# The second layer's modulation taken from TensorE to VectorE

## The reference, cut to what matters

```python
for i in range(DEPTH):
    mod_l = jnp.split((jax.nn.silu(c) @ w_mod[i] + b_mod[i])[:, None, :], N_MOD, axis=-1)
    mod_c = jnp.split((jax.nn.silu(c_ctx) @ w_mod[i] + b_mod[i])[None, None, :], N_MOD, axis=-1)
    h_l = modulate(rms_norm(x, norm1_g[i]), mod_l[0], mod_l[1])
    ...
    x = x + mod_l[2] * y_l
    x = x + mod_l[5] * squared_relu_mlp(modulate(rms_norm(x, norm2_g[i]), mod_l[3], mod_l[4]),
                                        w_mlp1[i], w_mlp2[i])
```

## Time and profile before

| what | value |
|---|---|
| median of 3 runs | 3845.44 us (3844.76 to 3845.57) |
| profiled execution, its own time | 3846.0 us |
| its span | 3843.8 us |
| PE busy | 3704.2 us, 96% of the span |
| DVE busy | 1794.8 us, 47% |
| ACT busy | 1378.0 us, 36% |
| mean granted clock of PE | 0.988 |

### The profile page before, as it was taken

The page is one execution under the profiler, slowest core; times in us unless marked ns, Lnnn a source line. Parts: engine busy times, 40 slices in busy tenths (PEclk is TensorE's granted clock), DMA queues, the critical chain, the costliest instruction groups (busy, mean ns, idle before and its releaser), DMA issues.

```text
span 3843.8 us, 65162 instructions
## 1 busy us (share of the span) xinstructions
PE 3704.2 (96%) x27522; PEld 3347.2 (87%) x27522; DVE 1794.8 (47%) x3203; ACT 1378.0 (36%) x2720; POOL 471.8 (12%) x570
## 2 busy tenths in 40 slices
PE   7999899999999999999999999999998999999998
PEld 7877778888888887888899889999997988999998
DVE  4544555233233556644455564443345556444444
ACT  3544444122123444422322352342233235234322
POOL 1122211000002432100011100110012110011001
PEclk9999999999999999999999999999999999999999
DMA  5111122232321211222311112222221111222222
GB/s 186 71 62 51 62 76 72 101 114 100 114 105 53 73 55 58 77 99 94 112 53 55 50 50 91 86 83 84 93 83 45 45 56 53 94 86 88 89 94 72
DMA packets 88128, 306.08 MB, mean 80 GB/s; under 512 B 10000, under 2 KB 13200, under 8 KB 87712
## 3 DMA queue, kind: packets, MB, share of 16 engines
q1 hardware_dynamic: 85184, 293.25, 21.7%
q0 software_dynamic: 2656, 8.68, 0.7%
HBM read 299.79 MB, written 2.10 MB: 79 GB/s over the span
## 4 chain that ended last, share of the span: by engine, by line
PE 90%; DVE 4%; ACT 3%; POOL 1%; issue 1%; DMA 0%; SPq 0%; POOLq 0%; DVEq 0%; ACTq 0%
PE bank L576 65%; PE bank L638 6%; PE bank L607 2%; PE bank L1089 2%; PE bank L875 2%; PE bank L914 1%; PE bank L1075 1%; PE bank L733 1%; PE bank L820 1%; PE bank L942 1%; PE bank L967 1%; PE bank L954 1%; DVE weight_lo L1870 1%; PE bank L1185 1%; PE bank L1213 1%
## 5 line engine op out<-in xcount | busy, mean ns | idle before, releaser
L1870 DVE TENSOR_TENSOR weight_lo<-weight_raw,weight_hi 128x1024 fp32r<-128x1024 f32 (+1 forms) x464 | 558.1, 1205 | 553.8 <-ACT weight_hi L1282 553.6
L1282 ACT ACTIVATE weight_hi<-weight_raw 128x1024 fp32r<-128x1024 f32 (+1 forms) x464 | 477.0, 1031 | 614.8 <-PE bank L576 371.1
L576 PE MATMUL bank<-u_hi,weight_hi 128*128 128x256 f32 (+1 forms) x2112 | 611.5, 290 | 2.5 <-DVE weight_lo L1870 2.3
L576 PE MATMUL bank<-u_lo,weight_hi 128*128 128x256 f32 (+1 forms) x2112 | 599.0, 284 | 0.0
L576 PE MATMUL bank<-u_hi,weight_lo 128*128 128x256 f32 (+1 forms) x2112 | 598.3, 283 | 0.0
L576 PE MATMUL bank<-h_hi,weight_hi 128*128 128x512 f32 (+1 forms) x1328 | 486.0, 366 | 16.0 <-DVE h_lo L2284 9.2
L576 PE MATMUL bank<-h_lo,weight_hi 128*128 128x512 f32 (+1 forms) x1328 | 466.5, 351 | 0.0
L576 PE MATMUL bank<-h_hi,weight_lo 128*128 128x512 f32 (+1 forms) x1328 | 465.9, 351 | 0.0
L576 PEld LDWEIGHTS bank<-u_hi,weight_hi 128*128 128x128 f32 x2112 | 399.6, 189 | 26.3 <-issue 20.8
L576 PEld LDWEIGHTS bank<-u_hi,weight_lo 128*128 128x128 f32 x2112 | 399.4, 189 | 0.0
L576 PEld LDWEIGHTS bank<-u_lo,weight_hi 128*128 128x128 f32 x2112 | 398.4, 189 | 0.2
(11 more groups left out here) (279 smaller groups left out, 7352.8 us busy)
## 6 DMA issues: line engine op xcount, KB each, us to landing
weight_raw<-in_w_mlp SPq DMA_DIRECT2D x128, 512.0 KB, 3.5
weight_raw<-in_w_ff SPq DMA_DIRECT2D x128, 512.0 KB, 3.5
weight_raw<-in_w_in SPq DMA_DIRECT2D x92, 512.0 KB, 3.5
weight_raw<-in_w_mod SPq DMA_DIRECT2D x80, 512.0 KB, 4.4
weight_raw<-in_a_w_qkv SPq DMA_DIRECT2D x24, 512.0 KB, 3.6
weight_raw<-in_b_w_qkv SPq DMA_DIRECT2D x24, 512.0 KB, 3.5
first_weight<-in_w_mod SPq DMA_DIRECT2D x16, 512.0 KB, 15.2
weight_raw<-in_w_ret_o SPq DMA_DIRECT2D x16, 512.0 KB, 3.4
```

The source lines that it names most:

```text
L576: m = e.matmul(view[:, 0:hi - lo], a[:, k, :], b[:, k0 + k, lo:hi], start=(k == 0 and i == 0), stop=(k == kt - 1 and i == 2))
L1282: e.activation(whi[s % N_SPLIT][:, 0:kt, :], raw[n % N_RAW][:, 0:kt, :], ACT.Copy).then_inc(*tick("act_split", ("hi", n)))
L1870: e.tensor_tensor(wlo[s][:, 0:kt, :], raw[n % N_RAW][:, 0:kt, :], whi[s][:, 0:kt, :].bitcast(F32), ALU.subtract).then_inc(*tick("dve_split ...
```

## The change

The layer-1 modulation leaves PE. The weights of layer 1's modulation are laid out on the host so that a tile holds 128 output columns, one on each partition, and along it the 1024 weights of that output. DVE multiplies such a tile by a row that holds the activated vector (the same on every partition) and sums the products along the row (`accum_out`), once for `c` and once for `c_ctx`. The products themselves go to scratch for the first and over the raw tile for the second; only the sums are used. The rows (`vector_rows`, 1 MB) are loaded by POOL after the attention of layer 0 and activated by ACT in one instruction of 128 x 2048. The bias is added once at the end. The side turns are 53 instead of 56. On DVE, the side turn is taken in front of the work on the running product's bank instead of behind it. The last ACT wait is there because the scratch of the products is the rows of squares that layer 1's norm uses.

```diff
+        CROWS = sb("vector_rows", [P, 2, D], F32, o_lcl)
+        PRODUCT = SCR[:, 4:6, :].rearrange("p a b -> p (a b)")[:, 0:D]
...
+            def modulation_loads(layer):
+                for m in range(6 * KT):
+                    done_with[weight((f"w_mod{layer}", m), split=False)] = ("modp", layer, m)
+                    yield
...
-            last = diffusion_layer(0, modulation(0, 2 * KT, 6 * KT, True),
-                                   paced(modulation(1, 0, 6 * KT, False), 6 * KT, 56))
+            last = diffusion_layer(0, modulation(0, 2 * KT, 6 * KT, True), paced(modulation_loads(1), 6 * KT, 53))
...
+            def vector_rows():
+                e.wait_ge(*at("crows"))
+                e.activation(CROWS[:, :, :], CROWS[:, :, :], ACT.Silu).then_inc(*tick("act_mod", ("crowss",)))
...
                 attention_layer(layer, side1)
+                if layer == 0:
+                    vector_rows()
                 def finish(q, m, span):
                     if q == 3 and layer == 0:
+                        e.wait_ge(*at("modp", 1, 6 * KT - 1))
                         square(("n1", 1), m, span, x_all(m, N_ALL), "xm", layer, q, m)
...
+            def modulation_rows(layer):
+                e.wait_ge(*at("crowss"))
+                for m in range(6 * KT):
+                    n = number[f"w_mod{layer}", m]
+                    w = raw[n % N_RAW][:, :, :].rearrange("p k c -> p (k c)")
+                    e.wait_ge(*at("raw", n))
+                    e.wait_ge(*at("modp", layer, m - 1))
+                    for s, to in enumerate((PRODUCT, w)):
+                        e.scalar_tensor_tensor(out=to, in0=w, scalar=1.0, in1=CROWS[:, s, :], op0=ALU.mult, op1=ALU.mult,
+                                               accum_out=mod_row(layer, m, s)).then_inc(
+                            *tick("dve_mod", ("modp", layer, m)))
+                    if m + 1 < 6 * KT:
+                        yield
+                e.wait_ge(*at("modp", layer, 6 * KT - 1))
+                both = MOD[layer][:, :].rearrange("p (m s) -> p m s", s=2)
+                e.tensor_tensor(both, both, vec("b_mod", 48 * layer, 48).unsqueeze(2).to_broadcast([P, 48, 2]),
+                                ALU.add).then_inc(*tick("dve_mod", *(("modd", layer, m) for m in range(6 * KT))))
+                yield
...
                         split_ahead(number[w1, KT * q + m])
+                        if q or m >= TURN:
+                            next(side, None)
                         j = m % 2
                         e.wait_ge(*at("relu", name, q, m))
...
-                        if q or m >= TURN:
-                            next(side, None)
...
                         split_ahead(number[w2, KT * q + m])
+                        next(side, None)
                         for span in range(len(tok.spans)):
                             finish(q, m, span, tok)
-                        next(side, None)
...
+                if layer == 0:
+                    e.dma_start(CROWS[:, :, :].rearrange("p s k -> p (s k)"), t["c_rows"]).then_inc(
+                        *tick("dma_crows", ("crows",), by=16))
                 turn(("n2", layer), KT)
...
-        out[f"w_mod{i}"] = tiles_of(a["w_mod"][i])
+        out[f"w_mod{i}"] = np.ascontiguousarray(a["w_mod"][i].T.reshape(-1, P, D)) if i else tiles_of(a["w_mod"][i])
```

More of the change, by code:

```diff
@@ L496, in mod, with mod_row @@
             return MOD[layer][:, j:j + 1]
+        def mod_row(layer, m, s):
+            return MOD[layer][:, 2 * m + s:2 * m + s + 1]
         def source(key):
@@ L1391, in modulation @@
                     e.wait_ge(*at("modp", layer, m0 + 1))
-                    e.wait_ge(*(at("modq", layer, m0 - 2) if m0 else at("modq", layer - 1, 46)))
+                    e.wait_ge(*at("modq", layer, m0 - 2))
                     e.activation(ROWS, view_of("mod", layer, m0)[:, 0:2 * P], ACT.Copy).then_inc(
@@ L1829, in scalar_program @@
             first_norm()
-            diffusion_layer(0, modulation(0, 2 * KT, 6 * KT, True),
-                            paced(modulation(1, 0, 6 * KT, False), 6 * KT, 56))
+            diffusion_layer(0, modulation(0, 2 * KT, 6 * KT, True), ())
             m0, w = KT - TURN, "b_w_qkv"
@@ L2675, in vector_program @@
             first_norm()
-            diffusion_layer(0, modulation(0, 2 * KT, 6 * KT, True),
-                            paced(modulation(1, 0, 6 * KT, False), 6 * KT, 56))
+            diffusion_layer(0, modulation(0, 2 * KT, 6 * KT, True), paced(modulation_rows(1), 6 * KT, 53))
             m0, w = KT - TURN, "b_w_qkv"
@@ L3153, in layout @@
     out["lambdas"] = np.ascontiguousarray(np.broadcast_to(lam.reshape(1, -1), (P, 4 * HD)))
+    both = np.stack([a["c"].reshape(-1), a["c_ctx"].reshape(-1)])
+    out["c_rows"] = np.ascontiguousarray(np.broadcast_to(both.reshape(1, -1), (P, 2 * D)))
     rows = lambda x: np.ascontiguousarray(x.reshape(-1, KT, P).transpose(2, 1, 0))
```

## The result

| | before | changed kernel |
|---|---|---|
| median | 3845.51 us | 3796.41 us |
| range of the executions (4 each) | 3844.76 to 3845.85 | 3793.54 to 3800.40 |
| ratio, 95% interval | | 0.9872 (0.9859 to 0.9885) |
| profiled execution | 3846.0 us | 3793.54 us |
| its span | 3843.8 us | 3791.6 us |

The kernel became 49 us faster, 1.3%.

A forecast was written before the change was run, and what follows sets the result against it. PE was taken to bound the MLP of layer 0, busy 482.00 of 482.00 us. 3846.0 - 39.4 (work leaving PE) + 1.0 (waits) = 3807.6, the median 0.6 lower, so 3807; range 3803 to 3818.

The forecast's parts named there:

- What leaves PE: MLP of layer 0 on PE: removing layer 1's modulation tiles and turnings saves 39.4 us, with a product at 8.46.
- What DVE gets: 96 products of 128 x 1024 with sums on DVE, taken as 2.65 us per pair.
- the lower end: Lowest price for a tile's pair of products on DVE, with free sums: 2 x 1.20 = 2.4 us.
- The first rival: DVE, L2067: sums run at half rate, a pair takes 4.9 us; time 3902, slower by 56; chance 0.12.
- Whether DVE keeps up: DVE's turns in the MLP: load is no limit, order is; PE waits 1 us, from 0 to 8.
- the ring: Waits through the raw buffer: DVE pair, SP load, ACT, DVE split, next pair; 8.66 us against a product's 8.46.
- the ring falls behind by 0.2 us per turn: MLP: ring 8.66 against product 8.46 uses up a lead of 1.8 us by the end of the first block.
- Beside the MLP: ACT's table load and Silu before the first Relu, and POOL's row load, are hidden, with 1.1 us to spare.
- the sum: Whole kernel: 3846.0 - 39.4 + 1.0 = 3807.6 us by the profiled execution; forecast 3807.
- The range: Whole kernel: 3803 to 3818 us, taking in the cheap part of the dearer sums; the forecast's own range 3804 to 3815.
- more switches saved: Fast end of the forecast's own range: more switches between kinds of matmul saved on PE and no wait, 3804 us.

The follow-up runs named there:

- the place undone: Changed kernel with DVE's side turn put back behind the work on the running product: 3886.61 us, ratio 1.0110.
- half tiles: Kernel before with four of eight matmuls in each of layer 1's 48 modulation tiles on TensorE: 3835.86 us, ratio 0.9975.
- the kernel without the work: Changed kernel without the layer-1 modulation's 96 products on DVE and its 48 tile loads: 3796.67 us, ratio 0.9870.
- without turnings: Kernel before without the 24 turnings of layer 1's modulation rows to columns on TensorE and VectorE: 3837.74 us, ratio 0.9980.
- the kernels with three and four: Changed kernel with three or four DVE products per tile instead of two, the first one repeated: 3833.75 us and 3893.55 us.

## Why the prediction was wrong, point by point

**What leaves PE** is the step that failed: "Two products with nothing between them take 16.92, so one is 8.46". They have nothing between them but stand between a tile and a turning, and so carry part of the price of both. Such a double product, here between two tiles, record by record in the kernel before:

```profile
739.89 0.50 PE L576 MATMUL bank<-h_hi,weight_hi 128*128 128x512 f32 x1
...
745.50 0.28 PE L576 MATMUL bank<-h_hi,weight_hi 128*128 128x256 f32 x1
...
748.38 0.40 PE L576 MATMUL bank<-h_hi,weight_hi 128*128 128x512 f32 x1
...
753.84 0.28 PE L576 MATMUL bank<-h_hi,weight_hi 128*128 128x256 f32 x1
...
756.80 0.65 PE L733 MATMUL bank<-weight_raw,odulation_or_window_mask 128*32 128x128 f32 x16
```

The 24 matmuls on 512 tokens take 5.61 behind a tile and 5.46 behind a product; those on 256 take 2.88 in front of a product and 2.96 in front of a tile. A bare product is 5.46 + 2.88 = 8.34, and so it is in the changed kernel, turn after turn:

```profile
645.94 0.40 PE L581 MATMUL bank<-h_hi,weight_hi 128*128 128x512 f32 x1
...
651.41 0.28 PE L581 MATMUL bank<-h_hi,weight_hi 128*128 128x256 f32 x1
...
654.28 0.40 PE L581 MATMUL bank<-h_hi,weight_hi 128*128 128x512 f32 x1
```

With 8.34 the prediction's own subtraction gives 495.24 - 54 x 8.34 = 44.9 and about 46 in all; 46.15 was measured. The term, 39.4, was 6.8 us too small, because the baseline was measured next to the thing whose price was sought. The rows for it were in the trace of before.

**What DVE gets**: the direction was right, the size of the pair was 2.37 instead of 2.65, and the lower end named (2.4) was the truth. The first rival is dead: no half rate.

**Whether DVE keeps up**: the waits of PE, taken as 1 us, were none. That is 1.0 of the miss. The links of the ring were right, and four kernels built on it came out as it says, but in the changed kernel it is shorter than its product. In the second turn the pair is done at 638.49, and then:

```profile
638.52 0.33 SPq L3054 DMA_DIRECT2D weight_raw<-in_w_mlp  x1
641.82 1.06 ACT L1293 ACTIVATE weight_hi<-weight_raw 128x1024 fp32r<-128x1024 f32 x1 [1.57 <-DMA weight_raw<-in_w_mlp]
```

With 0.03, 3.30, 1.09, 1.14 and a pair of 2.37 the ring is 7.93, where the prediction had 8.66; the first one, with 4.16 from issue to ACT, was 8.80, and the next six lie between 7.88 and 8.24. The lead of `weight_lo` over its product was smallest at the third product, 1.4 us, and grew from there, to 3.6 at the end of the first block; the prediction had it shrink from 1.8 to 0. So "the ring falls behind by 0.2 us per turn" was wrong too, and cost little since the prediction priced it at 1 us.

**Beside the MLP**: all of it hidden, as reckoned.

**What was not in the sum**: some 3 us by the medians (49.1 - 46.15), and 6.5 between the profiled executions, in stretches that the change does not touch. Both go with the granted clock. The norm turn takes 33.6 us at 1.00 (the changed kernel twice, the place undone), 35.1 to 35.2 at 0.95 (five profiles) and 35.9 to 36.2 at 0.90 or 0.91 (the kernel before, half tiles, and the kernel without the work). The rest takes 2633.9 to 2635.0 in four profiles (the changed kernel twice, without the work, with the place undone) and 2638.2 to 2638.8 in the other seven, the kernel before among them; by the clock's records in the traces PE spends 56 to 63 us of it at the 1.2 GHz level in the four, and 66 to 73 in the seven. The executions of one kernel differ in the same way: without turnings 3832.14 at 0.990 and 3840.07 at 0.987, with half tiles 3832.56 at 0.989 and 3837.63 at 0.986, while the 19 of the kernel before on one chip lie between 0.987 and 0.989 and within 4.3 us (3842.88 to 3847.13). The eight of the changed kernel range from 0.987 to 0.991 and over 11 us. What stays open is why the clock falls at one place in one execution and not in another, and why it varies more in the changed kernel.

**The range** was too narrow on the fast side for these two reasons: it allowed "more switches saved" and no wait some 3 us together, while the switches were 6.8 us more than reckoned, and it had nothing for the clock outside the stretch.

## What to carry to other kernels

To price work that sits between pieces of a saturated engine's main work, take the main work's bare duration from where it follows itself on both sides, record by record; the neighbours carry part of the price under their own line. An engine that is idle half of the time can still not take work anywhere: where a buffer ring ties its end to the next load, count the ring from buffer to buffer against the bounding engine's step, for both possible places. Here the place decided between 49 us faster and 41 us slower than the kernel before. And a few us between two executions are to be compared with their granted clocks before anything else is made of them.

## What the runs showed of the hardware

- A multiply with a sum over two fp32 inputs in SBUF, 128 x 1024, takes 1.22 us on DVE, no more than the subtraction of the same size (1.23); the read of the sum is a separate row of 0.08 us, beside the next instruction. The half rate that the Trainium skill gives for this form ("Vector Engine (DVE) Microarchitecture Reference", section "Points that are easy to get wrong") does not show in these 96 products, nor in the 144 and 192 of the kernels with three and four.
- On PE a change between a run of 128-column products with 32 columns of weights and the main products costs about 0.2 us for both sides together, beyond the rows of the small products themselves (0.57 us for 16 records, 0.36 for 8).
- Writing 96 x 512 KB of products into SBUF beside 119 GB/s of DMA did not make PE's 2880 matmuls longer: 503.18 us with all of it, 503.19 without.
- The same 182 matmuls behind the MLP took 33.6 us at a granted clock of 1.00, 35.1 to 35.2 at 0.95 and 35.9 to 36.2 at 0.90 or 0.91, in eleven profiles of ten kernels. A stretch of products in which PE never stopped had 1.00 throughout; the same products had 0.97 with 58.5 us of waits in them, and still 1.00 with 27.8 us.
